# A filler tensor of 480 bytes per partition cut to 96 bytes, in a decoder trunk on one core

## What is computed

```
h = x
for layer in range(DEPTH):                      # DEPTH = 2
    if layer == N_A_LAYERS:                     # 1
        kb, vb, kmean = shared_kv(h, kv_norm, w_kv)
    h = h + 0.5 * swiglu(rmsnorm(h, ffn1_norm[layer]), ffn1_w_in[layer], ffn1_w_out[layer])
    hn = rmsnorm(h, mix_norm[layer])
    if layer < N_A_LAYERS:
        h = h + s5_mixer(hn, ...)
    else:
        h = h + moba_attention(hn, w_q[j], w_o[j], kb, vb, kmean)
    h = h + 0.5 * swiglu(rmsnorm(h, ffn2_norm[layer]), ffn2_w_in[layer], ffn2_w_out[layer])
return rmsnorm(h, final_norm)
```

## Time and profile before

| | us |
|---|---|
| median of 3 runs | 1038.47 |
| lowest, highest | 1038.38, 1040.12 |
| the profiled execution's own time | 1038.38 |
| its span in the trace | 1036.6 |
| PE busy | 1000.9 (97%) |
| DVE, ACT, POOL busy | 606.8, 488.3, 233.6 |

### The profile page before, as it was taken

The page is one execution under the profiler, slowest core; times in us unless marked ns, Lnnn a source line. Parts: engine busy times, 40 slices in busy tenths (PEclk is TensorE's granted clock), DMA queues, the critical chain, the costliest instruction groups (busy, mean ns, idle before and its releaser), DMA issues.

```text
span 1036.6 us, 14378 instructions
## 1 busy us (share of the span) xinstructions
PE 1000.9 (97%) x5680; PEld 813.3 (78%) x5680; DVE 606.8 (59%) x756; ACT 488.3 (47%) x720; POOL 233.6 (23%) x291
## 2 busy tenths in 40 slices
PE   5999999898899999999999999999999999999996
PEld 4888888777688888888888888888855688888885
DVE  4676755669665555555655555545555465555543
ACT  6544444423455544445544444444543464444441
POOL 4999989879000000000000000000000000000000
PEclk9999999969999999999999999999975799999999
DMA  9766666500266566675566666666620165656651
GB/s 339 215 183 182 189 195 188 159 3 3 79 185 184 185 183 189 178 220 183 180 185 185 188 189 187 184 187 185 181 77 1 43 180 185 189 179 192 190 163 41
DMA packets 47890, 169.31 MB, mean 163 GB/s; under 512 B 5968, under 2 KB 5968, under 8 KB 47824
## 3 DMA queue, kind: packets, MB, share of 16 engines
q1 hardware_dynamic: 46368, 166.74, 53.3%
q10 hardware_dynamic: 1456, 1.66, 0.4%
HBM read 167.33 MB, written 1.05 MB: 162 GB/s over the span
## 4 chain that ended last, share of the span: by engine, by line
PE 92%; POOL 3%; DVE 2%; DMA 1%; ACT 1%; issue 1%; SPq 0%; DVEq 0%; POOLq 0%; ACTq 0%
PE ps L965 87%; PE ps L976 2%; POOL w_bd L440 1%; PE ps L1175 1%; DMA h<-in_x 1%; POOL c_bd L451 1%; PE ps L989 1%; POOL decay L458 1%; DVE w_lo L726 1%; PE ps L1074 0%; PE ps L1138 0%; PE ps L1002 0%; ACT act_out L618 0%; ACT act_out L539 0%; SPq L273 0%
## 5 line engine op out<-in xcount | busy, mean ns | idle before, releaser
L726 DVE TENSOR_TENSOR w_lo<-raw,w_hi 128x1024 fp32r<-128x1024 f32 x312 | 401.6, 1289 | 279.0 <-ACT w_hi L501 278.4
L501 ACT ACTIVATE w_hi<-raw 128x1024 fp32r<-128x1024 f32 x312 | 329.4, 1058 | 271.0 <-PE ps L965 271.0
L965 PE MATMUL ps<-w_hi,x_hi 128*128 128x512 f32 x896 | 354.8, 396 | 11.2 <-DVE w_lo L726 11.2
L965 PE MATMUL ps<-w_hi,x_lo 128*128 128x512 f32 x896 | 350.2, 391 | 0.0
L965 PE MATMUL ps<-w_lo,x_hi 128*128 128x512 f32 x896 | 349.7, 390 | 0.0
L965 PEld LDWEIGHTS ps<-w_hi,x_hi 128*128 128x128 f32 x896 | 168.8, 188 | 45.3 <-issue 11.0
L965 PEld LDWEIGHTS ps<-w_hi,x_lo 128*128 128x128 f32 x896 | 168.6, 188 | 36.0
L965 PEld LDWEIGHTS ps<-w_lo,x_hi 128*128 128x128 f32 x896 | 168.8, 188 | 33.7
L321 POOL TENSOR_TENSOR ms<-ss 128x2 f32<-128x2 f32 x7 | 1.4, 200 | 763.8 <-ACT act_out L539 762.4
L965 PE MATMUL ps<-w_hi,hid_hi 128*128 128x512 f32 x352 | 137.5, 391 | 0.0
L965 PE MATMUL ps<-w_hi,hid_lo 128*128 128x512 f32 x352 | 137.0, 389 | 0.0
(11 more groups left out here) (113 smaller groups left out, 705.2 us busy)
## 6 DMA issues: line engine op xcount, KB each, us to landing
raw<-in_in SPq DMA_DIRECT2D x176, 512.0 KB, 4.1
raw<-in_out SPq DMA_DIRECT2D x88, 512.0 KB, 3.6
raw<-in_glu SPq DMA_DIRECT2D x16, 512.0 KB, 4.2
raw<-in_k SPq DMA_DIRECT2D x8, 512.0 KB, 3.9
raw<-in_v SPq DMA_DIRECT2D x8, 512.0 KB, 4.4
raw<-in_q SPq DMA_DIRECT2D x8, 512.0 KB, 4.4
raw<-in_o SPq DMA_DIRECT2D x8, 512.0 KB, 4.2
xt<-in_xt SPq DMA_DIRECT2D x4, 256.0 KB, 5.9
```

The lines of the kernel that those rows point to most:

```text
L501: act.activation(w_hi[:, gu % WS, :], raw[:, gu % RAW, :], ACT.Copy)\
L726: dve.tensor_tensor(w_lo[:, gu % WS, :], raw[:, gu % RAW, :], w_hi[:, gu % WS, :].bitcast(F32), ALU.subtract)\
L965: return pe.matmul(o, w, x, start=start, stop=stop, skip_group_check=True)
```

## The change

The filler tensor shrinks from 120 to 24 float32 in each partition.

```diff
         rs = sb("rs", [P, TT])
 
-        sb("pad", [P, 120])
+        sb("pad", [P, 24])
```

## The result

The changed kernel took 1048.26 us (median of 6 runs, 1046.75 to 1051.07) against 1038.47 for the kernel before (6 runs beside it, 1034.93 to 1040.12). The ratio is 1.0099, with a 95% interval of 1.0077 to 1.012: it is slower by 9.8 us. The forecast was 1038.3 and no change. Where the record has the TensorE clock that a run was granted on average, it lies between 0.956 and 0.967 of full speed in all kernels here, and the runs at 0.959 or less are as a rule the longer ones of a kernel (see e12_after_again).

What follows compares the result with a forecast made beforehand. The prediction took PE's stream of line 965 products, about 227 ns each, as the bound. 1038.38 + 0 + 0 - 0.15 - 0.05 = 1038.2, against the median 1038.3 us, no change; range 1036.0 to 1040.8.

Steps and rivals of the forecast that it cites:

- rival B: Phases 1, 3, 4, 7, 8, 10, 12: weight loads of hid and x1 outlast their slot; 1043 to 1047 us, chance 0.08.
- the term for the weight loads: 2208 dense products with shifted hid or x1: running product hides the load; 0, bounds 8.8 us either way.
- A: Dense hid and x1 products: equal bases cause part of 14 ns, shifting gains up to 31 us; chance 0.10.
- C: PE's clock around 240, 270 or 815 us turns earlier or later, 2.4 us per 12 products; chance 0.03 each way.
- D: Whole kernel: the filler does nothing, all terms 0, 1038.4 us; chance 0.76 together with the forecast.
- Operands of the other engines: DVE, ACT and POOL accesses to shifted tensors on the chain: taken as 0, with 0.3 us either way.
- transfers at the start: Loads of xt and into w2 and tmp: new bases, 0.15 us sooner, between 0.3 sooner and 0.3 later.
- The transfers at the end: Last piece of fin, 2.1 us to land: 0.05 us sooner, bounds 0.2 us either way.
- The 10%: Start: landings into tmp 1.96 us apart, into w2 1.77; the difference used as bound on a transfer base's effect, either sign.
- The effect of 0.3 us: Transfers at both ends, by the descriptor rule: 0.2 us sooner at the start, 0.1 at the end, sum 1038.1.

Runs made afterwards that it cites:

- e12_after_again: The changed kernel unaltered, measured once more beside the kernel before: 1047.97 us against 1038.29, ratio 1.0099.
- e3_sweep_a: Against the kernel before, x0 moved to 0, hid to 384 and x1 to 192 modulo 512, weights staying at 128; 1052.97 us in one run.
- e8_s5_only: The changed kernel's shift of xt and the S5 tensors, with hid and x1 put back as before; 1036.43 us against 1036.36 for the kernel before.
- e1_hid_only: Against the kernel before, only hid_hi and hid_lo move, by +128 bytes; 1044.21 us against 1036.48, ratio 1.0066.
- e2_all_up: Against the kernel before, every tensor moves up by 128 bytes, the weights too; 1036.04 us against 1036.48, ratio 0.9992.
- e11: Against the kernel before, x0 and x1 at -16 bytes from the weights, hid at +16; 1035.55 us against 1038.29, ratio 0.9981.

## Why the prediction was wrong

**The reading of what bounds the kernel was right.** PE's stream of line 965 sets the time, and its pace is what a fraction of a percent hangs on. The count of products with a shifted stationary operand, 2208, was right, and so was the price of rival B from its point on: 2.2 us for each ns.

**The step that failed is the term for the weight loads.** It said: the load has 39 ns to spare in its slot, the running product hides it, so the term is 0. The runs show in its place that with the stationary operand at an unfavourable distance from the moving one the slot itself grows from 227.6 to 233.3 ns, while the load is still shown with 188 ns and 39 or 45 ns to spare. The spare was no cover, because the cost is not a longer load. 1152 products at 5.7 ns and 1056 at 5.5 to 6.3 are 12.4 to 13.2 us; the stages show 1.5 + 8.8 + 2.0 = 12.3, since some blocks run a little faster than the rest.

**Why the rows misled.** I bounded the term by the loads of hn against those of pr: two bases, 4 ns apart at most. Both were at half clock, and there the distance costs nothing (426.7 ns in e3_sweep_a at -128). The 4 ns belong to the two tensors and not to the base: with the bases exchanged by the change, hn keeps 230 ns and pr 226. I had compared the right thing under the one condition in which it can't be seen. And the three pairs with one pace were no three samples: before the change all of them had the distance 0. I had written that down, and then still counted "tensors at very different addresses" as evidence, when they differed only by multiples of 512.

**The rivals.** B named the place, the sign and the price, got 0.08, and its 1043 to 1047 ended a little below the 1048.3 measured. Its mechanism, a load later than its slot, isn't what the trace shows. A had seized on the right clue with the wrong sign: 14 ns of each product don't shrink with the clock, and I asked whether the distance of 0 caused them. It is the other way round: 0 is among the best distances, and moving off it raises those 14 ns to 20. C's clock did differ in the S5 part of the profiled executions, but kernels with unmoved distances show that difference too. D, that the filler does nothing, has fallen.

**The small terms.** Operands of the other engines and transfers at the start: together 0 within the interval (e8_s5_only, 1.0007, 0.9994 to 1.002). The transfers at the end, which that kernel leaves as they were, take 2.1 us to land before and after. The 10% that I read out of two gaps between landings was other traffic: in the changed kernel the bases are exchanged, and the gaps are 1.56 us for tmp and 1.91 for w2, so that the loads into w2 are still the ones further apart. The effect of 0.3 us that the prediction estimated from the Trainium skill, "DMA: Bandwidth & Descriptors", How a descriptor splits into AXI transactions, is too small for these intervals to show or to exclude.

The prediction also cited the Trainium skill, "SBUF — State Buffer", Who interferes with whom, by which PE's read ports for the moving operand and for the weight load are independent. The measurement differs: at full clock the pace goes from 227.0 to 232.4 ns when hid alone moves (e1_hid_only) and stays at 227.0 when the weights move with it (e2_all_up).

**What is shown and what isn't.** Shown: the cost sits in the dense products; it depends on the distance between stationary and moving operand modulo 256 (e2_all_up, and the pairs -64/+192 and 0/+256), not on the address itself; it goes on where the other engines are nearly idle and no transfer runs; it is absent at half clock; hid alone and x1 alone carry it, and the S5 tensors and the attention's add nothing that can be told. At equal granted clock the time follows the pace: 12.0 us for 12.3. The medians of the two single moves add up to 14.2 us, their runs at equal clocks to 11.0 to 13.3 (5.6 and 6.3, 5.4 and 7.0). Only argued: that load and stream meet in one bank of the memory. Open: which of the loads meets which stream, why -8 is slow and -16 fast, what the 14 ns at the best distance are, and the S5 part: it was 4.3 us shorter in the changed kernel's profile than in that of before; 2.6 to 2.8 of it is seen in kernels with the time of before as well, and where the rest comes from was not settled.

## What to carry to other kernels

Where PE runs such products (float32r, 128 x 128 stationary, 512 columns) back to back at full clock, the start of its stationary operand against that of its moving one is a tuning parameter: a filler of the wrong size ahead of either costs up to 3% of each product. Put both at the same residue modulo 256, and check it again after every change of an allocation, however dead the tensor. And a tensor that is never read isn't without effect: a table of addresses before and after, with the distances between operands of one instruction, belongs to the reading of such a diff.

## What the runs showed of the hardware

- At 2.4 GHz a product of 512 columns (float32r) repeats every 226.8 ns at best, not at half of the 427 ns of 1.2 GHz. The excess is 14 ns at the distances 0 and +-16 and 16 to 21 ns at all others that were tried.
- The effect repeats with 256 bytes, and it is already full at 4 or 8 bytes (232.5 and 233.3 ns).
- The S5 part took 72.7 to 73.2 us in the three profiles in which PE's clock stayed long at its lower level there (before, e1_hid_only and e3_sweep_a, 0.79 to 0.82 over 66 us) and 68.9 to 70.6 in the other eleven (0.87 to 0.92).
- The spread of a kernel's times goes with the granted clock of the whole execution. The 17 runs of before beside e11 have means of 1036.0 us at 0.965, 1038.5 at 0.958 and 1040.5 at 0.956. The three profiles with the long S5 part are those at 0.958 and 0.959.
